# Two changes of stage in a hybrid decoder step: semaphores kept, first loads moved ahead, output waits moved back

## The reference

```python
h = rmsnorm(x, norm_mix);  z = h @ w_in
q, k, v = l2norm / silu of a causal convolution over 4 tokens of parts of z
o, S    = gated_delta_rule(q, k, v, g, beta, S0)            # 6 heads, chunks of 64 tokens
hm, C   = mlstm_chunkwise(l_q, l_k, l_v, l_i, l_f, C0...)   # 6 heads, chunks of 64 tokens
ys      = s5_ssm(s_u, ...)                                  # complex state space, then GLU
x = x + concat(norm(o) * silu(gate), norm(hm) * sigmoid(l_o), s5_out) @ w_out
mk, mv  = rmsnorm(mem, norm_mem) @ w_xk, @ w_xv             # 256 memory tokens
x = x + cross_attn(rmsnorm(x, norm_x), mk, mv)              # 4 heads
x = x + square(relu(rmsnorm(x, norm_ff) @ w_ff1)) @ w_ff2   # 4096 hidden features
y = rmsnorm(x, norm_final)
```

## Time and profile before

| | us |
|---|---|
| runs | 1878.35 median of 3 (1874.34 to 1879.13) |
| profiled execution, its own time | 1874.03 |
| its span, first to last instruction | 1872.2 |
| TensorE busy / VectorE / ScalarE / GpSimd | 1765.1 / 653.2 / 523.9 / 415.2 |
| mean granted TensorE clock | 0.969 of full |

### The profile page before, as it was taken

One profiled execution on the slowest core, in us unless ns is written; L12 is line 12 of the kernel. 1 busy time (PEld: TensorE's weight loads), 2 busy tenths in 40 slices (PEclk: granted clock), 3 DMA queues, 4 the chain that ended last, 5 costly groups with the idle time before them and its releaser, 6 DMA issues.

```text
span 1872.2 us, 35836 instructions
## 1 busy us (share of the span) xinstructions
PE 1765.1 (94%) x15260; PEld 1551.5 (83%) x15260; DVE 653.2 (35%) x1282; ACT 523.9 (28%) x1177; POOL 415.2 (22%) x278
## 2 busy tenths in 40 slices
PE   6999989996989986999999999999999999999997
PEld 4666689996988985566667879999999999999997
DVE  7656567520444433513414361111111111111244
ACT  3443654211444432001124233201320032003211
POOL 1010223331122110000100004333333343334520
PEclk9999999997999997999999799999999999999999
DMA  3110011113232105700130001111111111111202
GB/s 137 51 36 23 24 46 44 46 37 57 33 76 34 27 16 208 270 0 0 68 129 7 1 1 57 40 51 45 45 35 52 49 45 38 52 45 45 79 16 78
DMA packets 52338, 100.28 MB, mean 54 GB/s; under 512 B 7744, under 2 KB 34736, under 8 KB 51952
## 3 DMA queue, kind: packets, MB, share of 16 engines
q1 hardware_dynamic: 51168, 96.25, 16.6%
q0 software_dynamic: 1040, 2.12, 0.4%
HBM read 90.18 MB, written 7.58 MB: 52 GB/s over the span
## 4 chain that ended last, share of the span: by engine, by line
PE 55%; DVE 2%; POOL 2%; ACT 1%; issue 0%; DMA 0%; POOLq 0%; DVEq 0%; ACTq 0%
PE ps L1989 13%; PE ps L1990 12%; PE ps L1991 12%; PE ps L1867 12%; PE ps L1972 1%; PE ps L1837 1%; PE ps L1830 1%; PE ps L1846 1%; PE ps L1901 1%; POOL feat_r L1811 1%; POOL regH_r L1813 0%; PE ps L1913 0%; DVE feat L2296 0%; PE ps L1925 0%; PE ps L1820 0%
## 5 line engine op out<-in xcount | busy, mean ns | idle before, releaser
L1989 PE MATMUL ps<-feat_r,rows_r 128*128 128x352 f32 x1392 | 451.1, 324 | 10.0 <-DVE feat_r L2354 8.1
L1991 PE MATMUL ps<-feat_r,regW_r 128*128 128x352 f32 x1080 | 346.8, 321 | 0.0
L1989 PEld LDWEIGHTS ps<-feat_r,rows_r 128*128 128x128 f32 x1392 | 261.8, 188 | 11.9 <-issue 9.3
L1990 PE MATMUL ps<-regH_r,rows_r 128*128 128x352 f32 x768 | 246.4, 321 | 0.0
L1991 PEld LDWEIGHTS ps<-feat_r,regW_r 128*128 128x128 f32 x1080 | 202.9, 188 | 0.0
L1990 PE MATMUL ps<-feat_r,rows_r 128*128 128x352 f32 x624 | 200.8, 322 | 0.0
L2162 ACT ACTIVATE feat<-ps 128x352 f32<-128x352 f32 x96 | 44.5, 464 | 484.5 <-PE ps L1991 484.4
L416 PE MATMUL ps<-regH,regW 128*128 128x352 f32 x528 | 164.5, 468 | 1.4 <-DVE regH L826 1.4
L2354 DVE TENSOR_TENSOR feat_r<-feat,feat_r (+1 forms) x96 | 53.1, 554 | 308.0 <-ACT feat_r L2166 308.0
L416 PEld LDWEIGHTS ps<-regH,regW 128*128 128x128 f32 x528 | 100.7, 194 | 57.6 <-issue 6.1
L1990 PEld LDWEIGHTS ps<-regH_r,rows_r 128*128 128x128 f32 x768 | 144.3, 188 | 0.2
(11 more groups left out here) (441 smaller groups left out, 2991.5 us busy)
## 6 DMA issues: line engine op xcount, KB each, us to landing
regW<-w_ff_in SPq DMA_DIRECT2D x45, 512.0 KB, 3.5
regW<-w_in_in SPq DMA_DIRECT2D x27, 512.0 KB, 3.5
regA<-xT_in SPq DMA_DIRECT2D x6, 1408.0 KB, 15.8
regA<-scr SPq DMA_DIRECT2D x80, 96.0 KB, 3.6
ext<-w_ff_in SPq DMA_DIRECT2D x15, 512.0 KB, 3.6
yT_out<-regA SPq DMA_DIRECT2D x12, 352.0 KB, 2.4
feat<-cv_in SPq DMA_DIRECT2D x8, 512.0 KB, 14.6
regH<-ck_in SPq DMA_DIRECT2D x8, 512.0 KB, 7.1
```

The lines of the kernel that those rows point to most:

```text
L1989: pe.matmul(bank[:, 0:BW], hi, rhs_hi(k, b), start=(k == 0), stop=False)
L1990: pe.matmul(bank[:, 0:BW], hi, rhs_lo(k, b), start=False, stop=False)
L1991: ins = pe.matmul(bank[:, 0:BW], lo, rhs_hi(k, b), start=False, stop=(k == KT - 1))
```

## The change

- No block of clears remains. Each stage allots semaphores with its own name suffix (`new_stage`). Those of stage A (`done_a`) are cleared by SyncE in stage B, behind the first round of row transfers; 32 names of stage C take over semaphores of stage B, and SyncE clears these behind its first two constants in stage C.
- SyncE asks for the constants in stage A, when the last convolution has left `ext` and the last silu has left `acc`, and for the first pair of rows of `bcG` and `bcB` when tile 24 is done. These buffers get fixed places: in `ext`, `acc` and, for `bcG` and `bcB`, in slots 0 and 1 of the weight ring.
- The memory tokens are loaded in stage B after the last token transposes (`tokm`).
- The wait for stage B's outputs moves into stage C, ahead of the wv load.

```diff
-        def clear_semaphores():
-            with nc.Block() as block:
-                @block.sync
-                def _(q):
-                    for name, s in sems.items():
-                        if name not in kept:
-                            q.sem_clear(s)
-            for name in [n for n in sems if n not in kept]:
-                nc.release_semaphore(sems.pop(name))
+        def new_stage(*carried):
+            kept = {n: sems[n] for n in carried}
+            left = [s for n, s in sems.items() if n not in carried + ("h0_in", "bc_in", "toep_in", "rows_in")]
+            sems.clear()
+            sems.update(kept)
+            stage[0] += 1
+            return left
...
+        colsel = ext[:, 804:864].rearrange("p (h t c) -> p h t c", h=2, t=2)
+        causal, causal4 = ext[:, 192:384]..., ext[:, 864:960]...
+        mvb = ext[:, 594:594 + NP * CNW]...
+        below = acc[:, 0:6 * CW]...
+        eye, seqs = acc[:, 840:904], acc[:, 904:904 + DB]
+        headsum = acc[:, 912:912 + NP * H]...
+        bcG, bcB = ([regW[:, k * KT * P + at:k * KT * P + at + NP * 2 * CW]... for k in range(2)]
+                    for at in (0, NP * 2 * CW))
... stage A, SyncE, after the last weight tile
+                sp_.wait_ge(sem("conv_ready"), CONV)
+                for name, ap in (("colsel", colsel), ("causal", causal), ("causal4", causal4)):
+                    sp_.dma_start(ap, const(name, ap)).then_inc(sem("k_in"), 16)
+                sp_.dma_start(mvb[:, :, CW:CNW], const("headsum", headsum)...).then_inc(sem("k_in"), 16)
+                sp_.wait_ge(sem("silu_ready"), 2 * CONV)
+                for name, ap in (("below", below), ("headsum", headsum), ("seqs", seqs)):
+                    sp_.dma_start(ap, const(name, ap)).then_inc(sem("k_in"), 16)
+                sp_.dma_start(eye, const("eye", eye)).then_inc(sem("eye_in"), 16)
+                sp_.wait_ge(sem("gemm"), turn(24, 2) + 1)
+                sp_.wait_ge(sem("scr_in"), 6 * 16)
+                spread(sp_, bcG, "g", 0, 0)
+                spread(sp_, bcB, "b", 1, 0)
                 sp_.wait_ge(sem("mend_ready"), 1)
                 sp_.dma_start(o["mend"], mend[0:6, :]).then_inc(sem("out_s"), 16)
                 sp_.wait_ge(sem("cnew_ready"), CONV)
                 sp_.dma_start(o["cnew"], cnew[:, :, :]).then_inc(sem("out_s"), 16)
-                sp_.wait_ge(sem("scr_in"), 6 * 16)
                 sp_.wait_ge(sem("out_s"), 48)
...
-        clear_semaphores()
+        done_a = new_stage("k_in", "eye_in", "g0", "b0")
... stage B, SyncE
-                (the constants, eye and the first pair of bcG and bcB)
-                spread(bcG, "g", 0, 1)
...
+                spread(q, bcG, "g", 0, 1)
                 for it in range(NC // 2 + 1):
...
+                    if it == 0:
+                        for s in done_a:
+                            q.sem_clear(s)
...
                 q.dma_start(demn, scr[5]).then_inc(sem("den_in"), 16)
+                q.wait_ge(sem("tokm"), NC + 1)
+                q.dma_start(memv, t["memT"]).then_inc(sem("mem_in"), 16)
...
-                q.wait_ge(sem("st_out"), 16 * (2 + DB))
...
-        clear_semaphores()
+        for s in done_a:
+            nc.release_semaphore(s)
+        spare = new_stage("mem_in", "st_out")
...
+        again = (the 32 names wq, wx, kc, vc, r, rl)
+        sems.update(zip(again, spare))
... stage C, SyncE
-                q.dma_start(memv, t["memT"]).then_inc(sem("mem_in"), 16)
                 q.dma_start(heads64, fixed("heads64")).then_inc(sem("cc_in"), 16)
                 q.dma_start(spread6, fixed("spread6")).then_inc(sem("cc_in"), 16)
+                for n in again:
+                    q.sem_clear(sem(n))
                 for n in range(XH):
                     q.dma_start(wk[n], t["w_xk"][n]).then_inc(sem("wk_in"), 16)
+                q.wait_ge(sem("st_out"), 16 * (2 + DB))
                 q.dma_start(regH[:, 4096:8192], t["w_xv"][0]).then_inc(sem("wv_in"), 16)
```

More of the change, by code:

```diff
@@ L121, in rounded @@
             return nc.alloc_sbuf_tensor_at(name + tag, shape, mybir.dt.float32r, offset=place[name])
[L123 removed]
+        sems, stage = {}, [0]
         def sem(name):
             if name not in sems:
[L127 removed]
+                sems[name] = nc.alloc_semaphore(name=f"{name}_{stage[0]}")
             return sems[name]
         scr = nc.dram_tensor("scr", (6, H, T), F32, kind="Internal").ap()
[L133 to L144 removed]
+        def new_stage(*carried):
[5 more added lines that the diff above has]
+            return left
         par = sb("par", [P, NPC])
@@ L215, in build, with const, spread @@
         h0 = sb("h0", [P, 2, ST, DB])
+        colsel = ext[:, 804:864].rearrange("p (h t c) -> p h t c", h=2, t=2)
+        causal, causal4 = ext[:, 192:384].rearrange("p (n m) -> p n m", n=NP), ext[:, 864:960].rearrange("p (n m) -> p n m", n=NP)
+        mvb = ext[:, 594:594 + NP * CNW].rearrange("p (n m) -> p n m", n=NP)
+        below = acc[:, 0:6 * CW].rearrange("p (l m) -> p l m", l=6)
+        eye, seqs = acc[:, 840:904], acc[:, 904:904 + DB]
+        headsum = acc[:, 912:912 + NP * H].rearrange("p (n m) -> p n m", n=NP)
+        bcG, bcB = ([regW[:, k * KT * P + at:k * KT * P + at + NP * 2 * CW].rearrange("p (n m) -> p n m", n=NP) for k in range(2)]
+                    for at in (0, NP * 2 * CW))
+        def const(name, ap):
+            w = ap.shape[1] if len(ap.shape) == 2 else int(np.prod(ap.shape[1:]))
+            return t["cst"][:, CC[name]:CC[name] + w]
+        def spread(q, tile, name, k, j):
+            w = 2 * CW if j < NC // 2 else DB * DS
+            for h in range(2):
+                src = scr[k, :, j * 2 * CW:j * 2 * CW + w].rearrange("(n h) t -> h n t", h=2)[h]
+                q.dma_start(tile[j % 2][64 * h:64 * h + 64, :, 0:w], src.unsqueeze(0).to_broadcast([64, NP, w]))\
+                    .then_inc(sem(f"{name}{j % 2}"), 16)
         resets = sb("resets", [P, DB * DS])
@@ L1028, in build @@
             return
-        clear_semaphores()
-        pools = [Carve(r) for r in (regA, regH, more, ext, acc, regW)]
+        done_a = new_stage("k_in", "eye_in", "g0", "b0")
+        pools = [Carve(r) for r in (regA, regH, more, ext[:, 0:192], ext[:, 384:594], ext[:, 960:1083], acc[:, 384:840])]
         def room(cols):
@@ L1047, in build @@
         L = 5
-        bcG, bcB, bcE, bcM, bcW = (mats(2, 2 * CW) for _ in range(5))
+        bcE, bcM, bcW = (mats(2, 2 * CW) for _ in range(3))
         S8 = room(DB * NP * CW).rearrange("p (b n m) -> p b n m", b=DB, n=NP)
@@ L1056, in build @@
         kbt, aT = mats(6), mats(6)
[L1057 to L1064, removed]
+        CN = ext[:, 384:594].rearrange("p (n m) -> p n m", n=NP)
+        pools[4].at = NP * CNW
+        R, vn, Sd, kw, eL, sT = (mats(1)[0] for _ in range(6))
+        RTd = mats(1, 32)[0]
         cols = room((NC + 1) * 15).rearrange("p (c q) -> p c q", q=15)
@@ L1067, in build @@
         den, demn = rows[32:38, 0, :], rows[32:38, 1, :]
-        def const(name, ap):
-            w = ap.shape[1] if len(ap.shape) == 2 else int(np.prod(ap.shape[1:]))
-            return t["cst"][:, CC[name]:CC[name] + w]
+        memv = zml[:, 6:9, :].rearrange("p k t -> p (k t)")[:, 0:KT * NMEM].rearrange("p (k t) -> p k t", k=KT)
         for n in ("k_in eye_in dn_zero ml_zero g0 g1 b0 b1 e0 e1 m0 m1 i0 i1 "
@@ L1143, in _ @@
             def _(q):
[L1144 to L1160, removed]
-                spread(bcG, "g", 0, 1)
-                spread(bcB, "b", 1, 1)
-                spread(bcM, "m", 3, 0)
-                spread(bcW, "i", 4, 0)
+                spread(q, bcG, "g", 0, 1)
+                spread(q, bcB, "b", 1, 1)
+                spread(q, bcM, "m", 3, 0)
+                spread(q, bcW, "i", 4, 0)
                 for it in range(NC // 2 + 1):
@@ L1696, in build @@
         FIRST = ((0, 0), (0, 1), (1, 0), (1, 1), (0, 2), (1, 2), (2, 0), (2, 1), (2, 2), (3, 0), (3, 1), (3, 2))
-        for n in ([f"wo{k}" for k in range(KT)] + [f"wq{k}" for k in range(XH)] + [f"wx{k}" for k in range(XH)] +
-                  [f"xr{k}" for k in range(NB)] + [f"kc{k}" for k in range(DB)] + [f"vc{k}" for k in range(DB)] +
-                  [f"r{k}" for k in range(4)] + [f"rl{k}" for k in range(4, KT)] +
+        again = ([f"wq{k}" for k in range(XH)] + [f"wx{k}" for k in range(XH)] + [f"kc{k}" for k in range(DB)] +
+                 [f"vc{k}" for k in range(DB)] + [f"r{k}" for k in range(4)] + [f"rl{k}" for k in range(4, KT)])
+        sems.update(zip(again, spare))
+        for n in ([f"wo{k}" for k in range(KT)] + [f"xr{k}" for k in range(NB)] +
                   "cc_in mem_in wk_in wv_in m_sq m_ps m_root m_h mix_sq mix_ss mix_v mix_root mix_r mix_g mix_bc mix_done dd_ready "
```

12 lines of the change are left out of this document (6 added, 6 removed).

## The result

The changed kernel takes 1852.68 us (median of 4 runs, 1851.55 to 1855.58) against 1876.34 beside it: a ratio of 0.9871, 95% interval 0.9854 to 0.9887. Timed again later it gave 0.9875 (0.9856 to 0.9894). The forecast was 1851. The profiled run took 1855.58 us over a span of 1853.8.

The account below looks back on a forecast made before the run. TensorE, busy 94% of the span, bounds the kernel, so time comes from two stage-change holes and the lower clock: 11.7 + 11.3 + 2.2 = 25.2 us off the middle run, 1876.2, gives 1851 us; 8-in-10 range 1842 to 1860.

Parts of the forecast that it names:

- First hole, 11.7 us: Between projection and chunk stage: the hole shrinks to one mark, TensorE starting 11.7 us sooner (10.9 to 11.9).
- Second hole, 11.3 us: Between chunk stage and memory stage: the hole ends one mark after the last state output, saving 11.3 us (10.5 to 11.5).
- Clears at 55 ns, marks at 0.3 us: In both holes: estimated prices of one SyncE semaphore clear, 55 ns, and of one closing mark, 0.3 us.
- The covers: Moved clears and loads hide behind existing waits: about 9 us for the 50 clears, at least 2.6 for the keys' weights.
- that rival: Third stage: the wk load lands last and takes 2 to 5 us of the gain, 1854.5 us; chance 0.10.
- The opening's clock, nothing: Chunk stage's opening: the clock still falls, a few us later; nothing counted, between -0.9 and +6.3 us.
- The first rival: Chunk stage's opening keeps the upper clock because the pause is gone: 6.3 us more, 1844.7 us; chance 0.10.
- The clock at the second boundary, 2.2 us: At the memory sums (L1820): the upper clock stays over a 1.8 us pause, gaining 2.2 us (0 to 2.4).
- The sum: Whole kernel: 11.7 + 11.3 + 2.2 = 25.2 us off, 1848.8 on the profiled time, 1851 us forecast.
- Slower: Chunk stage: the clock does not come back, deciding at about 521 us; held to 560 it gives 1892; chance 0.03.

Follow-up runs that it names:

- First only: Kernel before with only the first boundary changed (early constants and gate rows, no clears there), second boundary as before: 1865.63 us, ratio 0.9936.
- second only: Kernel before with only the second boundary changed (early memory rows, late output wait, no clears there), first as before: 1865.91 us, ratio 0.9942.
- both runs: Changed kernel with its 50 chunk-stage clears issued eight times, 1853.29 us; changed kernel with its 32 clears before the keys' weights issued ten times, 1865.26 us.
- the run that used it up: Changed kernel with the 32 clears ahead of the keys' weights issued ten times: 1865.26 us, ratio 0.9930 to the kernel before.
- opening filled: Changed kernel with seven and three unused matmuls in TensorE's pauses in the chunk stage's opening: 1855.20 us, ratio 0.9873 to the kernel before.
- gather early: Changed kernel with the 120 small gather matmuls put right behind the first chunk's products: 1849.00 us, again 1847.64, ratio 0.9850 to the kernel before both times.

## Why the prediction held, and where it did not

*First hole, 11.7 us.* Measured 11.76, by the mechanism given: the first matmul is released by the stage's mark, the loads having landed under the projection's last tiles. First only gives 12.0 us.

*Second hole, 11.3 us.* Measured 11.24; second only gives 10.9.

*Clears at 55 ns, marks at 0.3 us.* Long rows of clears gave 60 ns in both runs. With that, 79 clears are 4.74 us against 4.63 saved and 50 are 3.0 against 3.50, so a mark costs between nothing and 0.5 us. The sum over both blocks, 7.7 us by these prices, is 8.1.

*The covers.* Right in sign both times. The 50 clears had more cover than the 9 us forecast (350 added ones, 21 us, cost nothing). The keys' weights had 7.4 us of it in the run that used it up, at least 2.6 forecast. Their load did not take the place of the wait in the changed kernel, and that rival is out: what ends last before L1841 is VectorE's normalised memory, 1.13 us, as before.

*The opening's clock, nothing.* Right as a sum (21.24 against 21.07 us). The first rival, that a shorter pause keeps the upper clock, did not come true: 1.00 until 442, then 0.58 and 0.50, with pauses of 2.40 and 0.71 us. Filling these kept it up, so the lower clock there does hang on them: the mean granted clock from 437 to 462 is 0.66 to 0.73 in all six profiles that have both pauses and 1.00 in all four in which the long one is filled, by unused matmuls or by the gather. With the gather there the short one stayed (0.72 us), so the short one by itself does not lower the clock here. The Trainium skill, "TensorE: Matmul & The Clock Gate", has both sides: "The HAM clock gate" says that activity releases the lower clock, and "A second HAM failure mode: psum-queue depth-cycling" tells of a kernel whose short idle stretches between groups of matmuls made it swing. The opening, with one fall behind a pause of 2.40 us, is nearer to the second; of that page I had weighed only the first.

*The clock at the second boundary, 2.2 us.* This step failed. It said: "With the next work at 721.4 the pause is 1.8 us, and I expect the upper clock to stay". The pause was 1.84 us, and the clock fell: 0.58 from 709 to 717, and the sums took 6.42 us, in the second profile of the changed kernel 5.18, against 5.71 before. The gain was between -0.7 and +0.5 us. The two windows that it rested on, at 1386 and 1200, did not carry over to this place; they differ by 0.15 us of work, little to rest a forecast on. The price of the term was about right: where the clock stayed up the sums took 3.62 to 3.72 us (2.9 forecast), and from the last state output to the key projection it was 16.5 us (opening filled) against 18.2 (gather early) and 19.2 and 18.0 (changed kernel), 1.5 to 2.7 us. Its condition was wrong. In the kernel with the opening filled the clock stayed up over the same pause of 1.84 us, without a filler there, as its timeline and windows show:

```profile
712.93 3.72 PE L1835 MATMUL ps<-acc,cst 128*128 128x256 f32 x16 [1.84 <-ACT acc L2067]
```

```profile
708.00:717.00 9.00, 6.57 (x98) 5.48 (x93) 5.20 (x7) 4.17 (x10) 0.00 (x0) 1.00 0.61 190
```

Over that pause the clock fell in seven profiles and stayed up in this one; so the pause alone does not decide, and what does is open. The fillers show that it can be held, and that holding it there costs most of what it gives.

*The sum.* 25.2 us less the 2.2 that did not come is 23.0; the medians differ by 23.7. On the profiles' own times it is 18.4 (1874.03 to 1855.58, forecast 1848.8). There the output projection starts 25.2 us sooner, the very sum, but by luck (23.0, and 3.4 less 1.2 that the change did not make), and 6.8 us are lost behind it, where the sum expected all that follows to move along. *Slower*: the clock was back at 1.00 from 460, well ahead of the 521 at which that rival would have decided.

## What to carry to other kernels

Between two stages, ask what ends the hole and count it in rows: here 23.0 us were a list of clears (60 ns each), loads that could be asked for 30 to 40 us earlier, and a wait for outputs that nobody there needed. Such terms on SyncE's queue added up in these traces to about 0.1 us, and they move off the path when they stand where that queue waits anyway; test the cover by multiplying the moved work. When a hole closes, look at once at the order of the engine behind it: moving one group of matmuls into the next pause was worth 4 to 5 us more by the medians. When you reckon a cover, look up whether the wait is for the first of several loads or for the last. Do not book a clock gain on a pause being short; book it from a row in which the clock stayed up over that very pause, and look for where it is given back.

## What the hardware showed that I had not expected

Lower-clock stretches shift from run to run of one kernel, and the timings spread with them: two profiles of the changed kernel have memory sums of 6.42 and 5.18 us, and two of the gather-early kernel a value projection of 7.13 and 8.92; single executions of the latter lie between 1842.19 us, at a mean granted clock of 0.979, and 1854.21, at 0.973. The Trainium skill, "TensorE: Matmul & The Clock Gate", says in "The HAM clock gate" that how many matmuls run at the lower clock at a kernel's start varies between runs of one kernel; these rows show the like in its middle. A term of one or two microseconds that hangs on the clock can therefore be read in a trace and not in five rounds of timing.
